# First two weight slots of each sublayer as one 512-column moving operand

## The reference, cut to what matters

```python
# x: 256 tokens x 1024 features; four blocks of three sublayers, 12 in all:
# ffn ret ffn | ffn mla ffn | ffn stick ffn | ffn stick ffn
def _rmsnorm(x, g):
    return x * lax.rsqrt(jnp.mean(x * x, axis=-1, keepdims=True) + EPS) * g

def sublayer(x, pre, post, f, weight):
    return x + weight * _rmsnorm(f(_rmsnorm(x, pre)), post)

def swiglu(h, w_gate, w_up, w_down):          # w_gate, w_up: 1024 x 2816
    return (jax.nn.silu(h @ w_gate) * (h @ w_up)) @ w_down
...
```

## Time and profile before

| | |
|---|---|
| median of 3 runs | 1989.57 us (1988.1 to 1990.97) |
| the profiled execution, own time | 1989.47 us |
| its span, first to last instruction | 1987.7 us |
| PE matmul busy | 1949.2 us, 98% |
| DVE busy | 1205.6 us, 61% |
| ACT busy | 945.3 us, 48% |
| POOL busy | 155.6 us, 8% |
| DMA | 356.34 MB, mean 179 GB/s |
| mean granted TensorE clock | 0.999 |

### The profile page before, as it was taken

One profiled execution on the slowest core, in us unless ns is written; L12 is line 12 of the kernel. 1 busy time (PEld: TensorE's weight loads), 2 busy tenths in 40 slices (PEclk: granted clock), 3 DMA queues, 4 the chain that ended last, 5 costly groups with the idle time before them and its releaser, 6 DMA issues.

```text
span 1987.7 us, 33291 instructions
## 1 busy us (share of the span) xinstructions
PE 1949.2 (98%) x13704; PEld 1816.3 (91%) x13704; DVE 1205.6 (61%) x1194; ACT 945.3 (48%) x1035; POOL 155.6 (8%) x149
## 2 busy tenths in 40 slices
PE   7999999999999998999999999999999999999998
PEld 7999899999999997799999999989999999989998
DVE  4755656655665566665575556675556556666555
ACT  5433654533444456544454345753435344655433
POOL 3500122100000000100010001210001000200000
PEclk9999999999999999999999999999999999999999
DMA  8555544555555543365555555355555555535552
GB/s 297 201 181 189 180 160 146 194 172 187 190 193 188 190 146 133 117 201 190 181 189 181 189 191 191 128 190 191 180 182 196 183 190 183 194 129 185 181 182 102
DMA packets 262268, 356.34 MB, mean 179 GB/s; under 512 B 9008, under 2 KB 230576, under 8 KB 262192
## 3 DMA queue, kind: packets, MB, share of 16 engines
q1 hardware_dynamic: 258592, 342.15, 52.4%
q0 software_dynamic: 3600, 13.11, 1.8%
HBM read 354.19 MB, written 1.05 MB: 179 GB/s over the span
## 4 chain that ended last, share of the span: by engine, by line
PE 79%; ACT 4%; DVE 3%; issue 2%; POOL 0%; DVEq 0%; POOLq 0%; ACTq 0%
PE down L488 24%; PE bank L409 16%; PE bank L411 16%; PE bank L410 16%; PE bank L456 2%; DVE w_lo L1225 1%; ACT w_hi L882 1%; PE bank L448 1%; PE bank L447 1%; ACT h_hi L909 1%; DVE xn L1243 0%; DVE x L1276 0%; ACT junk L921 0%; PE bank L427 0%; PE bank L426 0%
## 5 line engine op out<-in xcount | busy, mean ns | idle before, releaser
L1219 DVE TENSOR_TENSOR w_lo<-raw,w_hi 128x2048 fp32r<-128x2048 f32 x311 | 712.7, 2294 | 412.1 <-ACT w_hi L882 412.1
L882 ACT ACTIVATE w_hi<-raw 128x2048 fp32r<-128x2048 f32 x322 | 615.5, 1912 | 490.8 <-PE down L488 249.9
L409 PE MATMUL bank<-h_hi,w_hi 128*128 128x256 f32 x2944 | 836.4, 284 | 0.0
L411 PE MATMUL bank<-h_hi,w_lo 128*128 128x256 f32 x2944 | 833.1, 283 | 0.0
L410 PE MATMUL bank<-h_lo,w_hi 128*128 128x256 f32 x2944 | 833.0, 283 | 0.0
L409 PEld LDWEIGHTS bank<-h_hi,w_hi 128*128 128x128 f32 x2944 | 564.7, 192 | 6.7 <-issue 2.9
L410 PEld LDWEIGHTS bank<-h_lo,w_hi 128*128 128x128 f32 x2944 | 564.7, 192 | 2.8
L411 PEld LDWEIGHTS bank<-h_hi,w_lo 128*128 128x128 f32 x2944 | 564.7, 192 | 0.0
L488 PE MATMUL down<-w_hi,m_hi 128*128 128x512 f32 x832 | 267.4, 393 | 0.7 <-DVE m_lo L1402 0.7
L488 PE MATMUL down<-w_lo,m_hi 128*128 128x512 f32 x832 | 264.7, 390 | 0.0
L488 PE MATMUL down<-w_hi,m_lo 128*128 128x512 f32 x832 | 264.4, 390 | 0.0
(11 more groups left out here) (214 smaller groups left out, 1442.8 us busy)
## 6 DMA issues: line engine op xcount, KB each, us to landing
raw<-in_ffn_w_gu SPq DMA_DIRECT2D x88, 1024.0 KB, 5.1
raw<-in_ffn_w_down SPq DMA_DIRECT2D x88, 1024.0 KB, 4.9
raw<-in_ffn_w_gate SPq DMA_DIRECT2D x44, 1024.0 KB, 5.3
raw<-in_ffn_w_up SPq DMA_DIRECT2D x44, 1024.0 KB, 5.3
raw<-in_w_in SPq DMA_DIRECT2D x20, 1024.0 KB, 5.1
raw<-in_ret_w_in SPq DMA_DIRECT2D x13, 1024.0 KB, 5.3
raw<-in_w_o SPq DMA_DIRECT2D x8, 1024.0 KB, 5.1
raw<-in_w_out SPq DMA_DIRECT2D x8, 1024.0 KB, 4.9
```

Of the source, the lines that this page charges most:

```text
L409: mm(o, w_hi[:, r, c:c + P], hi[:, k, :], start=(k == 0), stop=False)
L411: last = mm(o, w_lo[:, r, c:c + P], hi[:, k, :], start=False, stop=(k == KD - 1))
L882: act_fn(w_hi[:, r, :], raw[:, r, :], ACT.Copy).then_inc(hi_ready, 1)
L1219: v.tensor_tensor(w_lo[:, r, :], raw[:, r, :], w_hi[:, r, :].bitcast(f32), ALU.subtract).then_inc(lo_ready, 1)
```

## The change

`first_slots` now keeps a bank for each token half, and not for each slot: half 0 of both slots goes to the first bank, half 1 to the second. One matmul takes as moving operand 2 x 256 columns, the same feature block of both slots, out of two ring buffers (`both_slots`); where slot b+1 lies in a lower ring buffer than slot b, the sides in the bank are exchanged (`side_of`). The 96 matmuls of 256 columns become 48 of 512. The transposes of half 1 stand after 20 of the first 24, `second()` ahead of the second half. Both slots' high parts are needed at the start, and both slots are given back together, at the end (`slot_done` +2); a new count `first_half` tells that half 0 is done. The copies out of PSUM go by token half, in the feed-forward silu and product too (`silu_half`, `prod_half`), and PE's wait ahead of slot b+2 is for the first product. On DVE the two `low_half` become one `low(b+1)` ahead of `post_gained(u,1,1)`.

```diff
+
+        def side_of(n, s):
+
+            return s if n % RING < (n + 1) % RING else 1 - s
...
-            def first_slots(p, parts, hi=h_hi, lo=h_lo, second=lambda: None):
+            def both_slots(w, n, k):
+
+                r = sorted((n % RING, (n + 1) % RING))
+                return w[:, r[0]:r[1] + 1:r[1] - r[0], k * SC:(k + 1) * SC]
+
+            def high_both(n, bank, p, t, hi, lo):
+
+                pe.wait_ge(hi_ready, n + 2)
+                o, ts = bank[:, :].rearrange("p (a b) -> p a b", a=2), slice(t * P, (t + 1) * P)
+                for k in range(KD):
+                    if k % 4 == 0:
+                        pe.wait_ge(h_lo_done, 4 * p + 2 * t + k // 4 + 1)
+                    mm(o, hi[:, k, ts], both_slots(w_hi, n, k), start=(k == 0), stop=False)
+                    mm(o, lo[:, k, ts], both_slots(w_hi, n, k), start=False, stop=False)
+
+            def low_both(n, bank, t, hi, ks=range(KD)):
+
+                take(n + 1)
+                o, ts = bank[:, :].rearrange("p (a b) -> p a b", a=2), slice(t * P, (t + 1) * P)
+                for k in ks:
+                    last = mm(o, hi[:, k, ts], both_slots(w_lo, n, k), start=False, stop=(k == KD - 1))
+                return last
+
+            def first_slots(p, n, banks, hi=h_hi, lo=h_lo, second=lambda: None):


                 if p == 0:
                     turn(p, 0)
-                (n0, bank_a), (n1, bank_b) = parts
-                high_passes(n0, bank_a, p, 0, hi, lo)
-                low_pass(n0, bank_a, 0, hi)
+                high_both(n, banks[0], p, 0, hi, lo)
+                low_both(n, banks[0], 0, hi, range(KD // 2))
+                turn(p, 1)
+                low_both(n, banks[0], 0, hi, range(KD // 2, KD)).then_inc(first_half, 1)
                 second()
-                high_passes(n1, bank_b, p, 0, hi, lo)
-                turn(p, 1)
-                low_pass(n1, bank_b, 0, hi)
-                for n, bank in parts:
-                    high_passes(n, bank, p, 1, hi, lo)
-                    low_pass(n, bank, 1, hi).then_inc(slot_done, 1)
+                high_both(n, banks[1], p, 1, hi, lo)
+                low_both(n, banks[1], 1, hi).then_inc(slot_done, 2)
...
-                    first_slots(u + 1, [(b, bank0), (b + 1, bank1)], second=lambda: pe.wait_ge(evac, evacs[0]))
+                    first_slots(u + 1, b, gemm_bank, second=lambda: pe.wait_ge(evac, evacs[0]))
...
-                    pe.wait_ge(silu_done, e + 1)
+                    pe.wait_ge(prod_half, ffns + 1)
...
+            def first_out(t, n, p, dsts):
+
+                sc.wait_ge(*((first_half, p + 1) if t == 0 else (slot_done, n + 2)))
+                if p:
+                    sc.wait_ge(pre_rs, 2 * p + t + 1)
+                bank = gemm_bank[evacs[0] % 2]
+                for dst, s, c0, c1 in dsts:
+                    at = side_of(n, s) * SC
+                    last = act_fn(dst, bank[:, at + c0:at + c1], ACT.Copy, scale=scale_of(t) if p else 1.0)
+                last.then_inc(evac, 1)
+                evacs[0] += 1
...
-                    sc.wait_ge(slot_done, b + 1)
-                    sc.wait_ge(pre_rs, 2 * (u + 1) + 2)
                     wait(sc, prod_done, e)
+                    at = side_of(b, 0) * SC
                     for t in range(T):
-                        last = act_fn(silu_g[:, t * S:(t + 1) * S], bank0[:, t * S:(t + 1) * S], ACT.Silu, scale=scale_of(t))
-                    last.then_inc(silu_done, 1)
+                        sc.wait_ge(*((first_half, u + 2) if t == 0 else (slot_done, b + 2)))
+                        sc.wait_ge(pre_rs, 2 * (u + 1) + t + 1)
+                        act_fn(silu_g[:, t * S:(t + 1) * S], gemm_bank[t][:, at:at + SC], ACT.Silu, scale=scale_of(t)).then_inc((silu_half, silu_done)[t], 1)
...
+                            elif j < 2:
+                                first_out(j, b, u + 1, [(r_v[:, j, s * SC:(s + 1) * SC], s, 0, SC) for s in range(2)])
+                                if j == 1:
+                                    row_copy()
                             elif j < 3:
                                 rows_out(b + j, u, [(r_v[:, :, j * SC:(j + 1) * SC], 0, SC)])
-                                if j == 1:
-                                    row_copy()
...
-                        rows_out(b, u, [(c_nat[:, :, 0:QR], 0, QR)])
+                        first_out(0, b, u + 1, [(c_nat[:, 0, 0:QR], 0, 0, QR), (c_nat[:, 0, QR:QR + KVR], 1, 0, KVR), (kr[:, 0, :], 1, KVR, KVR + ROPE)])
                         high(b + 3)
-                        rows_out(b + 1, u, [(c_nat[:, :, QR:QR + KVR], 0, KVR), (kr, KVR, KVR + ROPE)])
+                        first_out(1, b, u + 1, [(c_nat[:, 1, 0:QR], 0, 0, QR), (c_nat[:, 1, QR:QR + KVR], 1, 0, KVR), (kr[:, 1, :], 1, KVR, KVR + ROPE)])
...
                 pre_low(u + 2, 0)
                 post_gained(u, 1, 0)
+                low(b + 1)
                 post_gained(u, 1, 1)
-                low_half(b + 1, 0)
                 post_add(u, 1)
                 pre_scale(u + 2, 1)
-                low_half(b + 1, 1)
                 pre_low(u + 2, 1)
...
-                    ve.wait_ge(silu_done, e + 1)
-                    ve.wait_ge(slot_done, b + 2)
+                    at = side_of(b, 1) * SC
                     for t in range(T):
+                        ve.wait_ge(*((silu_half, ffns + 1) if t == 0 else (silu_done, e + 1)))
                         h = slice(t * S, (t + 1) * S)
-                        last = v.scalar_tensor_tensor(act[:, h], bank1[:, h], stat[:, 4 + t:5 + t], silu_g[:, h], ALU.mult, ALU.mult)
-                    last.then_inc(prod_done, 1)
+                        v.scalar_tensor_tensor(act[:, h], gemm_bank[t][:, at:at + SC], stat[:, 4 + t:5 + t], silu_g[:, h], ALU.mult,
+                                               ALU.mult).then_inc((prod_half, prod_done)[t], 1)
                     low(b + 3)
                     low(b + 4)
```

More of the change, by code:

```diff
@@ L215, in build @@
         hi_ready, lo_ready = sem("hi_ready"), sem("lo_ready")
-        slot_done = sem("slot_done")
+        slot_done, first_half = sem("slot_done"), sem("first_half")
+        silu_half, prod_half = sem("silu_half"), sem("prod_half")
         silu_done, prod_done = sem("silu_done"), sem("prod_done")
@@ L445, in high_passes @@
                     if k % 4 == 0:
                         pe.wait_ge(h_lo_done, 4 * p + 2 * t + k // 4 + 1)
-                    mm(o, hi[:, k, ts], w_hi[:, n % RING, c:c + SC], start=(k == 0), stop=False)
-                    mm(o, lo[:, k, ts], w_hi[:, n % RING, c:c + SC], start=False, stop=False)
-            def low_pass(n, bank, t, hi):
-                take(n)
-                o, ts = bank[:, t * S:(t + 1) * S], slice(t * P, (t + 1) * P)
+                    mm(o, hi[:, k, ts], w, start=(k == 0), stop=False)
@@ L454, in low_pass @@
+                    mm(o, lo[:, k, ts], w, start=False, stop=False)
+            def low_pass(n, s, bank, t, hi):
+                take(n + s)
+                o, ts = bank[:, side_of(n, s) * SC:(side_of(n, s) + 1) * SC], slice(t * P, (t + 1) * P)
                 for k in range(KD):
-                    c = k * SC
-                    last = mm(o, hi[:, k, ts], w_lo[:, n % RING, c:c + SC], start=False, stop=(k == KD - 1))
-                return last
-            def first_slots(p, parts, hi=h_hi, lo=h_lo, second=lambda: None):
+                    last = mm(o, hi[:, k, ts], w_lo[:, (n + s) % RING, k * SC:(k + 1) * SC], start=False, stop=(k == KD - 1))
+                return last
@@ L610, in _ @@
             pe.wait_ge(const_in, 16)
-            first_slots(0, [(n, next_bank()) for n in range(2)], m_hi, m_lo)
+            first_slots(0, 0, [next_bank() for t in range(T)], m_hi, m_lo)
             take(2)
@@ L661, in _ @@
                     mem = list(mem_heads(0, 0))
-                    first_slots(u + 1, [(b + j, next_bank()) for j in range(2)])
+                    first_slots(u + 1, b, [next_bank() for t in range(T)])
                     spread_scale(u)
@@ L1002, in _ @@
                     pre_high(1, 0)
-                copy_out(n, (mv if n < 2 else mk_T)[:, n % 2, :, :])
+                if n < 2:
+                    first_out(n, 0, 0, [(mv[:, s, n, :], s, 0, SC) for s in range(2)])
+                else:
+                    copy_out(n, mk_T[:, n % 2, :, :])
                 high(n + 3)
@@ L1147, in _ @@
                         for j in range(2):
-                            rows_out(b + j, u, [(s_v[:, :, j * SC:(j + 1) * SC], 0, SC)])
+                            first_out(j, b, u + 1, [(s_v[:, j, s * SC:(s + 1) * SC], s, 0, SC) for s in range(2)])
                             if j == 1:
```

8 lines of the change are left out of this document (4 added, 4 removed).

## The result

The changed kernel takes **1992.86 us** (median of 20 runs, 1991.48 to 1994.61), the kernel before 1989.6 (20 runs on the same chip, 1988.1 to 1991.72). The ratio is 1.0017, 95% interval 1.0010 to 1.0023: 3.3 us slower, less than the 0.2% that was set as the bound, but clear of noise, since the interval does not reach 1. The forecast was 1.3 us faster: the time lies in the range, the sign is wrong.

What follows compares the result with a forecast made beforehand. PE, busy 1949.2 of 1987.7 us, was taken as the bound. Ten boundaries at -0.3, mla +1.45 and start +0.25 gave -1.3 us from the profiled 1989.47, so 1988.2 us; range 1984.0 to 1994.0.

Steps and rivals of the forecast that it cites:

- The boundary: Between sublayers: half 1 would end at 561.0 in place of 561.31, a gain of 0.3 us at each of ten boundaries.
- 0.05 for the semaphore: At a boundary: time added after `h_lo`, whose 0.68 us ends the chain 2.03 us after half 1's transposes.
- The start: Launch to first feed-forward: PE starts later, on both high parts; +0.25 us after `first_slots` gives back 0.6.
- If the slow pace lasts as long again: At the start: the slow first 3.60 us would recur and cover 8.5 wide matmuls, putting the transposes at 23.8 us.
- it ends 0.85 late: At the start: half 1 begins at 25.8 in place of 24.68 and, less 0.31, ends 0.85 us late.
- The bound of +1.7: At the start: upper bound of its term, if the slow pace lasts twice as long; the lower was -0.65.
- The mla term: In mla: `high(b+3)` stands ahead of the second copy and delays the squares; +1.45 us, the boundary's own gain included.
- No cost: After the products: slots b+3 and b+4 convert later, with 1.7 us of cover for b+3; costed at nothing.
- Rival (b): At eleven boundaries POOL's root misses its 0.12 us margin and `post_add` starts 0.5 late: +5.5, 1993.7 us; chance 0.12.
- Rival (a): At ten boundaries half 1's chain is quicker or PE less bound by it: 0.45 us each, 1983.7 us; chance 0.14.
- (c): Slots given back 2.3 us later empty the conversions, so PE waits for slot b+3: 1994 us; chance 0.04.
- Rival (d): Wide matmuls over two ring buffers cost as two narrow ones, 0.240 us; half 1 keeps nothing: 1992.2 us; chance 0.10.

Runs made afterwards that it cites:

- e4: Kernel before, with VectorE's whole `low(b+1)` put ahead of half 1's `post_gained`, in place of two halves: 1991.54 us.
- e3: Changed kernel, with half 1 of the two slots done by 48 narrow matmuls in place of 24 wide ones: 1996.3 us.
- e12: Kernel before, with identity transposes where PE waits, 12 at the start and 18 in mla: 1989.6 us.
- e10: Changed kernel, with identity transposes where PE waits, 24 at the start, 20 and 18 at two mla waits: 1990.56 us.
- e8: Changed kernel, in mla with `high(b+3)` behind the squares, its low part behind the scaling, `high(b+4)` behind the copies of the transposes: 1990.55 us.
- e2: Changed kernel, in mla with the second copy out (half 1) ahead of `high(b+3)`: 1992.84 us.
- e1: Changed kernel, with half 0 of the memory part's two slots at the start in the old order with narrow matmuls: 1992.72 us.
- e6: Changed kernel, with `low(b+1)` in halves: first ahead of half 0's subtraction, second between half 1's two gain products: 1988.96 us.
- e13: Kernel before, with the low part's first half ahead of half 0's subtraction, second between the gain products, no wide operand: 1987.3 us.
- e11: Changed kernel with e6's halves, e8's mla order and identity transposes, 24 at the start and 20 at mla's second wait: 1984.1 us.
- e14: Same as e11 but without the 20 identity transposes in mla: 1985.92 us.

## Why the prediction was wrong

**The boundary** is the step that failed by most: "Gain 0.3 us at each boundary". Measured are 0.11, -1.12 for ten in place of -3.0. The mechanism was right: VectorE's steps came within 0.03 us of the working (5.62 for the transposes, where 5.65 stood), and so did the wait of about 1 us. Two small things were mis-sized. Half 1 waits for `h_lo`, and "0.05 for the semaphore", for which no row was named, was 0.15: the first half of `h_lo` ends at 556.78, half 1 starts at 556.93. So it began at 7.78 and not at 7.68, 2.16 us behind the transposes and not 2.03. And half 1 itself took 5.57 and not 5.45, since behind the wait its first interval is 0.31 and the next ones 0.232. Each is 0.1 us, and the gain was only 0.3. e4 and e3 give the same by another way: +0.15 for VectorE's order, -0.27 for half 1's columns.

**The start** comes second: +0.25 was predicted, +1.52 measured. The step is "If the slow pace lasts as long again", and with it "it ends 0.85 late"; the end of the memory part's products came 1.96 late (32.47 against 30.51). The 3.6 us were read from a table that ends where a group of eight matmuls begins; the group itself was slow to its middle, 4.5 us in all, and in after it was 5.3. The transposes came at 24.82, not at 23.8, half 1 at 26.93, not at 25.8. The rest of the step held. Half 0 of the first feed-forward starts 10.01 us behind the start of ScalarE's last conversion ahead of it (the row under e12), in before (33.09 and 43.10) as in after (35.08 and 45.09), so nothing of the 1.96 was hidden; and its `first_slots` took 12.31 in place of 12.80 and gave back 0.49, where 0.6 stood. By e10 the fast pace brings the first mark back to 227.61, so 1.8 us hang on the pace. The bound of +1.7 did hold the term.

Part of the +1.52 is luck of these two launches. With after's start, word for word, the slow stretch ended at 21.2 us in e8's trace and at 23.2 in e2's, and their first marks are 228.68 and 229.49. In e8's it lasted 3.5 us, as the prediction took it: half 1 at 26.15, the first mark 0.77 behind before's. With before's start e4, whose weights landed 1.3 us later, shows a first mark of 229.26, where before has 227.91. A single pair of traces gives the start's term no better than to about a microsecond, and how the runs without a trace started is not known.

**The mla term** was right: +1.45 predicted, +1.73 measured. The squares came 2.74 us behind the start of `high(b+3)` (2.8). The missing 0.3 is the boundary gain that was counted into it and did not come: with the start and the intervals ahead of it taken off (1.18 us), `high(b+3)` began at 752.06 and not at 751.78. e8 takes 1.34 us of it away.

**No cost** was right for slots b+3 and b+4: no wait there. Rival (b) did not come: the root ended at 552.60, 0.11 ahead of `post_add`, at the predicted margin of 0.12. Rival (a) neither, nor (c). Rival (d) is excluded by e3.

**The sum** of the three terms as measured is -1.12 + 1.73 + 1.52 = +2.13, and 0.43 behind the last mark: 2.56, the difference of the profiled executions. Against the forecast of -1.3 the boundaries make up 1.9 us, the start 1.3, mla 0.3 and the end of the run 0.4. The other 0.7 us of the median are runs with more of the lower clock: of after's 20 runs ten show a mean granted clock of 0.999 (1991.48 to 1992.3) and ten 0.997 (1993.41 to 1994.61). That these are longer or further falls in mla is likely by e1's profile, where the clock was 0.996; it is not shown, as after has one trace, and that is of a run with 0.999.

## What to carry to other kernels

A wait that goes from a list is worth only what the next late thing allows: here `w_lo` and `xn` were both due 6.64 us after half 0, and neither order of VectorE could gain before both came earlier (e6, e13). Pairing two slots halves the matmuls, but it also makes both slots' first work wait for both conversions and gives both back at once, so look at what stands behind the first slot: at the start and in mla that cost more than ten boundaries gained, even with the start as short as in e8's trace. Where a term is a tenth of a microsecond times ten, measure the restart after a wait and not only the pace in the middle of a loop. And a term from the first microseconds of a launch wants more than one trace.

## What the runs showed of the hardware

- TensorE's first matmuls run at half pace: 0.212 us for 256 columns, 0.427 for 512, until 20.25 us in before and 22.99 in after, where the trace has its first entry of the clock, of full speed; the 1.00 that is printed for the time ahead of it misleads. With the same instructions the stretch lasted from 3.5 us (e8) to 5.7 (e2). With 12 or 24 transposes put into the wait ahead of them (e10, e11, e12, e14) that entry stands at 14.5 to 15.4 us, and the matmuls ran at 0.12 and 0.23 from the first or second on.
- In the mla sublayer the clock fell to the 1.2 GHz level in 13 of the 14 profiles, and the place and length were not the kernel's alone: at 761 us for 3.4 in before, 763.7 for 3.4 in after, 760.5 and 781 for 6.8 each in e1, 779 for 6.8 in e4, 803.5 for 3.4 in e12, and not at all in e13, whose stream there is before's. With a wait filled it fell later in e10, e11 and e12, but in e4, with none filled, it fell late too; so what the filling did to the place is not shown, only that falls still came.
- A 128 x 1 operation of GpSimd that took 0.54 us beside a VectorE operation that reads PSUM took 2.04 beside `low(b+1)`, both of whose inputs lie in SBUF, and ended 0.41 us behind it, as the earlier trace rows had shown for its sibling. The Trainium skill (SBUF — State Buffer, two separate sides) has an operation of VectorE with two SBUF inputs and one of GpSimd that reads SBUF lock out each other for a whole instruction; by that rule the trace of after agrees.
